# GpSimd takes the bias of the convolution's norm and the low weights of every second memory unit there

## What is computed

```python
u = causal_depthwise_conv(u, conv_w, conv_b)
u = jax.nn.silu(layer_norm(u, conv_ln_g, conv_ln_b))     # (512, 1024)
...
return jnp.concatenate([u, y], axis=-1) @ w_out           # mixer's output
...
k = (mem @ w_k)                                           # 256 x 1024, cross-attention
v = (mem @ w_v)
```

## Time and profile before

| | |
|---|---|
| median of 3 runs | 2525.89 us (2525.19 to 2527.41) |
| the profiled execution, own time | 2524.29 us |
| its span in the trace | 2522.5 us |
| TensorE's mean granted clock | 0.996 of 2.4 GHz |
| busy: PE, DVE, ACT, POOL | 2471.1, 1699.1, 1294.5, 404.4 us |

### The profile page before, as it was taken

The page is one execution under the profiler, slowest core; times in us unless marked ns, Lnnn a source line. Parts: engine busy times, 40 slices in busy tenths (PEclk is TensorE's granted clock), DMA queues, the critical chain, the costliest instruction groups (busy, mean ns, idle before and its releaser), DMA issues.

```text
span 2522.5 us, 38409 instructions
## 1 busy us (share of the span) xinstructions
PE 2471.1 (98%) x15181; PEld 2144.2 (85%) x15181; DVE 1699.1 (67%) x3249; ACT 1294.5 (51%) x2558; POOL 404.4 (16%) x476
## 2 busy tenths in 40 slices
PE   7999999999999999999999999999999999999998
PEld 6876677899988978778897999889898887999888
DVE  5476977688863499997774988535635744987533
ACT  4365554367742435564654687424534453677422
POOL 2233342200000156553000100000000100100000
PEclk9999999999999999999999999999999999999999
DMA  9532234434443233223421333332321442333332
GB/s 285 136 93 71 63 101 121 132 99 126 118 126 98 80 101 94 58 67 95 131 84 51 92 111 108 96 96 82 93 76 34 134 126 59 85 111 107 93 99 86
DMA packets 455092, 253.29 MB, mean 100 GB/s; under 512 B 16458, under 2 KB 449310, under 8 KB 454911
## 3 DMA queue, kind: packets, MB, share of 16 engines
q1 hardware_dynamic: 451615, 243.18, 33.7%
q0 software_dynamic: 3152, 7.59, 1.2%
q10 hardware_dynamic: 144, 0.07, 0.0%
HBM read 247.99 MB, written 2.80 MB: 99 GB/s over the span
## 4 chain that ended last, share of the span: by engine, by line
PE 84%; DVE 10%; ACT 3%; issue 2%; DMA 1%; SPq 0%; POOL 0%; DVEq 0%; ACTq 0%; POOLq 0%
PE ps L1134 15%; PE ps L1136 15%; PE ps L1142 15%; PE ps L1199 4%; PE ps L1201 4%; PE ps L1204 4%; PE ps L1049 4%; PE ps L1051 4%; PE ps L1047 4%; PE ps L1375 2%; PE ps L1232 1%; DVE ps L3034 1%; PE ps L1229 1%; PE ps L1227 1%; PE ps L1720 1%
## 5 line engine op out<-in xcount | busy, mean ns | idle before, releaser
L1950 ACT ACTIVATE wh<-w_f 128x512 fp32r<-128x512 f32 (+2 forms) x621 | 351.1, 614 | 337.7 <-PE ps L1142 158.1
L2914 DVE TENSOR_TENSOR w_r<-w_f,wh 128x512 fp32r<-128x512 f32 (+1 forms) x459 | 295.9, 688 | 334.1 <-ACT wh L1950 333.6
L1134 PE MATMUL ps<-XH,wh 128*128 128x512 f32 (+1 forms) x1136 | 458.0, 403 | 4.4 <-ACT wh L1950 3.5
L1136 PE MATMUL ps<-XL,wh 128*128 128x512 f32 (+2 forms) x1016 | 398.0, 392 | 0.2 <-DVE XL L3434 0.2
L1142 PE MATMUL ps<-XH,w_r 128*128 128x512 f32 (+2 forms) x1160 | 309.2, 390 | 1.1 <-DVE w_r L2914 0.8
L1136 PE MATMUL ps<-arena_r,wh 128*128 128x512 f32 (+1 forms) x808 | 297.1, 373 | 0.1
L4213 POOL TENSOR_TENSOR w_r<-w_f,wh 128x256 fp32r<-128x256 f32 (+1 forms) x314 | 236.1, 782 | 352.2 <-ACT wh L1950 352.2
L1134 PEld LDWEIGHTS ps<-XH,wh 128*128 128x128 f32 (+1 forms) x1136 | 211.9, 186 | 69.2 <-issue 16.0
L1142 PEld LDWEIGHTS ps<-XH,w_r 128*128 128x128 f32 (+2 forms) x1160 | 215.5, 186 | 51.2 <-DVE w_r L2914 3.2
L1136 PEld LDWEIGHTS ps<-XL,wh 128*128 128x128 f32 (+2 forms) x1016 | 189.5, 186 | 42.8 <-issue 1.7
L1134 PE MATMUL ps<-arena_r,wh 128*128 128x512 f32 (+1 forms) x568 | 210.6, 379 | 0.8 <-ACT wh L1950 0.8
(11 more groups left out here) (499 smaller groups left out, 5913.4 us busy)
## 6 DMA issues: line engine op xcount, KB each, us to landing
w_f<-in_mlp_w SPq DMA_DIRECT2D x126, 512.0 KB, 4.0
w_f<-in_w_ff SPq DMA_DIRECT2D x63, 512.0 KB, 4.1
w_f<-in_w_in SPq DMA_DIRECT2D x49, 512.0 KB, 3.9
w_f<-in_ada_w SPq DMA_DIRECT2D x35, 512.0 KB, 4.0
w_f<-in_even_w_in SPq DMA_DIRECT2D x35, 512.0 KB, 3.8
w_f<-in_odd_w_in SPq DMA_DIRECT2D x23, 512.0 KB, 3.7
w_f<-in_even_w_out SPq DMA_DIRECT2D x16, 512.0 KB, 3.9
w_f<-in_xa_w_v SPq DMA_DIRECT2D x16, 512.0 KB, 3.3
```

What stands on the lines that cost most here:

```text
L1134: e.matmul(b, hi[:, k, :], xh, start=u.first and k == 0, stop=False)
L1136: e.matmul(b, hi[:, k, :], xl, start=False, stop=False)
L1950: e.activation(high_flat(u)[:, s], flat(u, 0)[:, s], ACT.Copy).then_inc(act.sem, act.up("high", u.n, i))
L2914: e.tensor_tensor(low[:, s], raw_[:, s], high[:, s], ALU.subtract).then_inc(dve.sem, dve.up("low", u.n, i))
```

## The change

It does three things. The bias of the convolution's norm goes from ScalarE to GpSimd: eight instructions of 128x512. ScalarE's tanh and VectorE's silu wait for it. Every second one of the 12 units gets `low` = "pool". And GpSimd's program gets the walk through `plans["conv wait"]` and the norm's loop that it didn't need before.

```diff
+    late_kv = plans["conv wait"] + [u for k in range(KC) for u in plans["conv norm", k]]
+    for u in late_kv[::2]:
+        u.low = "pool"
...
             def conv_silu(k):
-                w.wait_ge(dve, "norm", "conv", k)
-                e.activation(conv[:, k, :], conv[:, k, :], ACT.Identity, bias=column("even_conv_ln_b_2", k)).then_inc(
-                    act.sem, act.up())
                 s, freed = sil.take("u", k)
                 w.wait_ge(*freed)
-                w.wait_ge(act, act.count)
+                w.wait_ge(pool, "biased", "conv", k)
                 e.activation(s, conv[:, k, :], ACT.Tanh, scale=0.5).then_inc(act.sem, act.up("u tanh", k))
...
             def conv_silu(k):
                 s = conv[:, k, :]
                 w.wait_ge(act, "u tanh", k)
+                w.wait_ge(pool, "biased", "conv", k)
...
             conv_inputs("conv wait")
+            for u in plans["conv wait"]:
+                lower_ahead(u.n)
+            for k in range(KC):
+                w.wait_ge(dve, "norm", "conv", k)
+                e.tensor_scalar(conv[:, k, :], conv[:, k, :], column("even_conv_ln_b_2", k), None, ALU.add).then_inc(
+                    pool.sem, pool.up("biased", "conv", k))
+                for u in plans["conv norm", k]:
+                    lower_ahead(u.n)
```

## The result

The changed kernel took 2532.72 us, the median of 16 runs (2527.69 to 2538.25), against 2524.77 of the kernel before in the same sessions (16 runs, 2519.34 to 2527.88). Between the medians that is 8.0 us. The ratio over all runs is 1.0036 (9.1 us), with a 95% interval of 1.0026 to 1.0046: the change makes the kernel slower, by somewhere between 6.6 and 11.6 us. The two figures differ because single runs scatter over some 10 us. The profiled execution took 2532.49 us, 8.2 more than that of the kernel before.

The account below looks back on a forecast made before the run. VectorE's list up to its `out` pair piece was taken to bound the stretch: 7.7 + 2.9 - 4.8 - 0.9 + 1.1 = +6.0 us, +7.3 with the clock, giving 2533.2 us; range 2527.0 to 2538.5.

Parts of the forecast that it names:

- ScalarE's 5.9 us are worth at most 0.9: Norm's loop: removing eight biases from ScalarE frees 5.9 us there, but at most 0.9 us of VectorE's tanh waits.
- the decisive piece: VectorE's low-weights piece for the `out` pair behind the norm's loop; its time was said to set the stretch's end.
- VectorE is spared 4.8 us: Norm's loop: eight low pieces leave VectorE at 0.60 us each, 4.8 us in all.
- Ahead of the loop balanced, from a gain of 1.2 to a loss of 0.5: Before the last tap: VectorE's saved pieces balance GpSimd's collisions; bounds, gain of 1.2 us to loss of 0.5.
- 16 pieces for 7.7 us by taking turns: Norm's loop: each GpSimd low piece costs VectorE 0.48 us by contention, 7.7 us for 16.
- Rival 5: Norm's loop: turns cost little, under 0.21 us a piece, and the lighter lists win; 2523.5 us, 8%.
- Seven biases for 2.9 us: Norm's loop: each GpSimd bias before VectorE's `out` piece costs VectorE 0.42 us, 2.9 us in all (1.5 to 8.1).
- Rival 2: Norm's loop: a GpSimd bias costs VectorE as much as a two-input sum; +12.5 us, 2538.4 us, 11%.
- the prediction's own sign: GpSimd's bias in the loop: a duration of 1.3 us was to show the dear-bias rival instead of the forecast.
- The first unit +1.1 and the tanh waits -0.9: Norm's loop: late first GpSimd low weights idle VectorE 1.1 us (0 to 2.2); its 0.9 us of tanh waits go.
- The clock, +1.3: Behind the `out` pair: longer TensorE waits drop its clock for 3 us, costing 1.3 us (0 to 1.5).
- The sum of VectorE's way: VectorE's work and waits up to its `out` piece behind the loop: forecast +6.0 us, without the clock.

Follow-up runs that it names:

- e11: Kernel before with the norm's bias left out altogether (ScalarE's eight instructions and the wait behind them); 2522.61 us, ratio 0.9998.
- e2: Changed kernel with the bias back on ScalarE; every second unit's low weights stay on GpSimd; 2526.36 us, ratio 1.0006.
- e3: Kernel before with only the low weights of two units ahead of the norm's loop moved to GpSimd; 2525.64 us, ratio 1.0002.
- e1: Changed kernel with all low weights back on VectorE, only the bias on GpSimd; 2530.75 us, ratio 1.0027.
- e6: Kernel before plus eight bias instructions on GpSimd, on scratch, for which nobody waits; 2527.14 us, ratio 1.0014.
- e5: Changed kernel with the real bias back on ScalarE and GpSimd's bias on scratch, nobody waiting for it; 2529.74 us against 2522.45, ratio 1.0023.
- e9: Changed kernel with the first of the loop's GpSimd units back on VectorE; 2529.06 us against 2524.45, ratio 1.0019.
- e7: Kernel before with low weights of four units in a row, all made ahead of the norm's loop, on GpSimd; 2523.07 us against 2522.45, ratio 1.0001.
- e10: Changed kernel measured and profiled again, nothing altered; 2532.99 us against 2524.45 of the kernel before, ratio 1.0045.
- e8: Kernel before plus seven GpSimd instruction forms on scratch, each once in the norm's loop and once behind it; single run, 2525.19 us.
- e4: Changed kernel with a constant 0.5 in place of the bias's per-partition column; 2532.86 us, ratio 1.0036.
- e12: Changed kernel with GpSimd's bias as a sum of two tensors, the column broadcast along the row; 2530.39 us, ratio 1.0039.

## Why the prediction was right, and where it wasn't

2533.2 us were predicted and 2532.72 measured, slower, by the mechanism named as likeliest. That the numbers agree so closely is partly luck: the forecast stood on a median of before of 2525.89, which was 2524.77 over 16 runs, and added 7.3 us where the medians lie 8.0 apart and the ratio says 9.1. Term by term, in the order of the prediction:

- *ScalarE's 5.9 us are worth at most 0.9:* right, 0.7 (e11). Of the two tanh waits that make the 0.9, only that of 0.65 us stands ahead of the decisive piece; the other, 0.29, comes behind it (at 1241.1) and didn't belong in the sum.
- *VectorE is spared 4.8 us:* right; e2's way is that with its collisions.
- *Ahead of the loop balanced, from a gain of 1.2 to a loss of 0.5:* a loss of 0.5 (e3), the bad end. VectorE's two remaining pairs took 1.6 us longer there.
- *16 pieces for 7.7 us by taking turns:* 8.2 (e2). Rival 5, which needed under 0.21 us a piece, is refuted by 0.51.
- *Seven biases for 2.9 us:* 2.8 (e1, e6), though the bias is nothing like the affine select on GpSimd, 2.46 us beside VectorE. The price for VectorE was right, and the prediction gave it without seeing that GpSimd's own time is another number. Rival 2 tied a dear bias to 1.15 us for VectorE: by the prediction's own sign, a bias at 1.3 us, rival 2 would hold, for the bias takes 1.56 us or more; but it didn't cost VectorE what rival 2 says, so the sign was ill chosen. With both together in the changed kernel the collisions are 9.2 us and not 11.0 (8.2 + 2.8). That some fall into VectorE's new idle time is shown for one bias (at 1222.14, 1.56 us) and argued for the rest.
- *The first unit +1.1 and the tanh waits -0.9:* this is the part of the sum that came out wrong. Net +0.2 was forecast for VectorE's waits, and they grew by 3.5 us (0.65 to 4.16). The wait behind the first unit is 2.42, beyond the upper bound of 2.2, since the bias ahead of the four pieces took 1.94 us and they were through 7.1 us after the first norm began (1222.15 less 1215.09), where the forecast had about 6.2 (1218 less 1211.8). With 0.27 us ahead of another unit's low weights it makes 2.69. And the tanh waits didn't go, they came anew, 1.46 us of them (0.43 and 1.03): a bias queued behind four pieces of 1.1 us lets ScalarE wait up to 3.6 us, and VectorE's silu behind it. That the pieces' place behind the bias makes the wait of 2.42 is shown by e5, which keeps it, and by e9, in which it goes. The tanh waits fall to 0.36 in e5, but the way stays as long.
- *The clock, +1.3:* a fall behind the pair cost 1.7 us in both traces of the changed kernel. A second one of 1.7 was in the first trace alone. The reason given for it was wrong: the two waits at the pair were to grow to some 2 and 3 us, 4 to 5 in sum, and they are 1.55 and 1.17, 2.72 in sum. In the kernel before and in e7 waits of 1.62 and 0.77 had no fall behind them, so this term was right by luck.

The sum of VectorE's way: 9.2 - 4.8 + 3.5 = +7.9, where 6.0 was forecast; with the last tap's 0.5 that is +8.4, against 8.2 measured without falls. With one fall +9.9 (e10), with two +11.5. The medians say +8.0 and, in the session of e10, +8.5; the ratios 9.1 and 11.4, with intervals that reach 11.6 and 15.9. The forecast of +7.3 hit the medians; against the stretch with one fall it was 2.6 us too small, and its +6.0 without the clock 2.1 to 2.2.

The Trainium skill, page SBUF — State Buffer, section SBUF: two separate sides, says that the loser blocks until the winner's whole instruction is done. The runs disagree: a GpSimd instruction of 2.46 us held VectorE for 0.41 (e1, e6). Its section Who interferes with whom says that a VectorE instruction with at most one SBUF input, outside the two-port modes, doesn't contend with GpSimd; the taps of e7, with one operand in PSUM, agree at 0.67 us each.

## What to carry to other kernels

Price a move to GpSimd twice: once by what it reads (about 0.4 us of VectorE's time for 512 columns of one tensor here, twice that for two), and once by its own duration beside a busy VectorE, which was 1.2 to 1.9 times that alone for the adds by a column or constant, the copy and the broadcast sum and about four times for the select and the plain sum, and sets how late everything queued behind it comes. Put such work where VectorE reads PSUM; there it was free for both (e7). And when an execution's total and the changed stretch disagree, compare two markers on either side of the change.

## What the runs showed of the hardware that I had not expected

- A per-partition add of 128x512 in float32 on GpSimd took 1.56 us beside a resting VectorE (the changed kernel) and 2.46 beside two-input instructions (e1, e6, e8); with a constant 1.49 and 1.86; the copy 0.61 and 1.01 (e8).
- The loss of VectorE was 0.41 or 0.42 us for each of these, whatever their length, and 0.84 for a broadcast sum that was itself shorter (1.42 us).
- Waits of TensorE between 2.15 and 2.19 us, at the same place in the program, were followed by a fall of the clock in one trace and by none in six (e2, e3, e4, e9, e10, e12): here the length of the wait alone doesn't decide it. Likewise in the loop: a wait of 2.65 us for the first unit had no fall behind it in three traces (the changed kernel's two, e5), waits of 2.37 (e4) and 2.40 (e12) had one.
- The same 105 us of work went 4% slower in some executions than in others, at a granted clock of 1.00 in both: 894 matmuls for 929, at one place in seven of 14 traces (before, e1, e2, e3, e4, e7, e10). The cause is open.
